# A decoder layer on one core: weight sums of column pair 1 moved behind a token split, down-projection sums moved two column pairs on, stores of f moved ahead

## What is computed

```python
h = rms_norm(x, pre_ffn_w[l]) * (1.0 + scale2) + shift2
u = causal_dwconv(h @ w_up[l], ffn_conv_w[l], ffn_conv_b[l])      # 1024 -> 2 * 2816, 3 taps
u_gate, u_val = jnp.split(u, 2, axis=-1)
f = (jax.nn.gelu(u_gate, approximate=True) * u_val) @ w_down[l]   # 2816 -> 1024
x = x + gate2 * rms_norm(f, post_ffn_w[l])
```

## Time and profile before

| | |
|---|---|
| median of 3 runs | 1133.82 us (1129.49 to 1134.27) |
| the profiled execution | 1129.23 us, of which 1127.2 us are its span |
| PE busy | 1075.1 us, 95% of the span |
| DVE busy | 871.6 us, 77% |
| ACT busy | 560.5 us, 50% |
| POOL busy | 253.3 us, 22% |
| mean granted TensorE clock | 0.983 |

### The profile page before, as it was taken

One profiled execution on the slowest core, in us unless ns is written; L12 is line 12 of the kernel. 1 busy time (PEld: TensorE's weight loads), 2 busy tenths in 40 slices (PEclk: granted clock), 3 DMA queues, 4 the chain that ended last, 5 costly groups with the idle time before them and its releaser, 6 DMA issues.

```text
span 1127.2 us, 14880 instructions
## 1 busy us (share of the span) xinstructions
PE 1075.1 (95%) x5096; PEld 865.0 (77%) x5096; DVE 871.6 (77%) x1121; ACT 560.5 (50%) x1012; POOL 253.3 (22%) x237
## 2 busy tenths in 40 slices
PE   4699999999998999889999999999999999999997
PEld 3578766666686888767888888888888888888885
DVE  5869677767559687799888888888888877776687
ACT  4821254545554556565554445445444545544453
POOL 2000011121125443133333333333333100000012
PEclk7799999999999999999999999999999999999999
DMA  9979411001134222235353535343433595623324
GB/s 345 321 245 318 139 38 38 20 20 38 57 114 133 92 94 75 76 93 165 115 167 112 167 112 167 109 164 118 153 107 123 206 391 196 213 94 96 100 85 168
DMA packets 117503, 157.40 MB, mean 140 GB/s; under 512 B 15308, under 2 KB 76237, under 8 KB 117453
## 3 DMA queue, kind: packets, MB, share of 16 engines
q1 hardware_dynamic: 117133, 155.69, 41.3%
q0 software_dynamic: 320, 1.06, 0.3%
HBM read 125.75 MB, written 30.98 MB: 139 GB/s over the span
## 4 chain that ended last, share of the span: by engine, by line
PE 77%; DVE 11%; ACT 4%; DMA 2%; issue 2%; POOL 1%; SPq 1%; DVEq 0%; POOLq 0%; ACTq 0%
PE ps L2451 33%; PE ps L2518 18%; PE ps L2121 18%; DVE big L1409 3%; DMA raw<-in_w_in_dram 2%; PE ps L2160 2%; PE ps L2186 1%; PE ps L2174 1%; DMA scratch<-in_rel_bias_dram 1%; PE ps L2291 1%; DVE w_lo L1450 1%; PE ps L2077 1%; PE ps L2219 1%; POOL st L766 1%; DVE a_lo L1743 0%
## 5 line engine op out<-in xcount | busy, mean ns | idle before, releaser
L2121 PE MATMUL ps<-a_hi,w_hi 128*128 128x512 f32 x416 | 141.9, 419 | 7.5 <-DVE a_lo L1469 3.8
L2121 PE MATMUL ps<-a_lo,w_hi 128*128 128x512 f32 x416 | 131.6, 395 | 0.0
L2121 PE MATMUL ps<-a_hi,w_lo 128*128 128x512 f32 x416 | 131.0, 393 | 0.0
L2518 PE MATMUL ps<-w_hi,a_hi 128*128 128x512 f32 x308 | 119.9, 389 | 0.2 <-DVE a_lo L1953 0.2
L2518 PE MATMUL ps<-w_lo,a_hi 128*128 128x512 f32 x308 | 119.8, 389 | 0.0
L2518 PE MATMUL ps<-w_hi,a_lo 128*128 128x512 f32 x308 | 119.8, 389 | 0.0
L1321 ACT ACTIVATE w_hi<-raw 128x512 fp32r<-128x512 f32 x77 | 48.7, 632 | 98.4 <-PE ps L2518 88.8
L2121 PEld LDWEIGHTS ps<-a_hi,w_hi 128*128 128x128 f32 x416 | 72.7, 191 | 29.4 <-issue 16.3
L2121 PEld LDWEIGHTS ps<-a_lo,w_hi 128*128 128x128 f32 x416 | 78.9, 190 | 17.7
L2121 PEld LDWEIGHTS ps<-a_hi,w_lo 128*128 128x128 f32 x416 | 78.7, 189 | 17.9
L1238 ACT ACTIVATE scratch<-ps 128x512 f32<-128x512 f32 x88 | 52.0, 593 | 80.6 <-PE ps L2451 80.5
(11 more groups left out here) (270 smaller groups left out, 2398.5 us busy)
## 6 DMA issues: line engine op xcount, KB each, us to landing
big<-in_w_ada_dram SPq DMA_DIRECT2D x20, 1024.0 KB, 8.8
raw<-in_w_up_dram SPq DMA_DIRECT2D x23, 512.0 KB, 5.0
big<-in_w_down_dram SPq DMA_DIRECT2D x22, 512.0 KB, 6.2
down_weight_sums<-big SPq DMA_DIRECT2D x22, 512.0 KB, 3.4
raw<-down_weight_sums SPq DMA_DIRECT2D x44, 256.0 KB, 2.8
ffn_hidden<-big SPq DMA_DIRECT2D x21, 512.0 KB, 2.6
big<-ffn_hidden SPq DMA_DIRECT2D x21, 512.0 KB, 7.5
big<-in_w_up_dram SPq DMA_DIRECT2D x20, 512.0 KB, 4.9
```

Of the source, the lines that this page charges most:

```text
L2121: mm = pe.matmul(out, lhs_of[a], rhs_of(b, j), start=first and p == 0, stop=last and p == 2)
L2518: mm = pe.matmul(bk, a[:, ts], rhs_op(s)[w], start=fresh and m == 0, stop=last and m == 2, skip_group_check=s // KH in (J6, J3, J7))
```

## The change

Three edits. POOL waits, before the weight sums of pair 1, until the low part of b22 REST is made. DVE makes the sums of w_down number 0 in pair 2 instead of pair 1; number 1 stays in pair 3. SP stores f of the pair before ahead of the stores and loads for the sums, in all pairs.

```diff
--- before.py
+++ after.py
@@ -658,12 +658,12 @@
                     sp.wait_ge(s_ul, weights_to(p, "a22"))
                     sp.wait_ge(s_us, 4 if first else p * 2 + 2)
                     load_pair(p + 2, par)
+                if not first:
+                    store_f(p - 1)
                 if par == 0 and not first:
                     store_sums(i - 1)
                 if par == 1 and not last:
                     load_sums(i)
-                if not first:
-                    store_f(p - 1)
@@ -858,6 +858,7 @@
+            pool.wait_ge(s_bl, splits_to("b22", REST))
             weight_sums(1, 1)
             with pool.Fori(1, FT // 2) as i:
                 for par in range(2):
@@ -1969,8 +1970,10 @@
             next_weights(1, 1)
             assemble(0, 0, 1)
 
-            up_pair(1, 1, sums=0)
-            with dve.Fori(1, FT // 2 - 1) as i:
+            up_pair(1, 1)
+            up_pair(2, 0, sums=0)
+            up_pair(3, 1, sums=1)
+            with dve.Fori(2, FT // 2 - 1) as i:
                 for par in range(2):
                     up_pair(i * 2 + par, par, sums=i if par else None)
             up_pair(FT - 2, 0, sums=KH - 1)
```

## The result

The changed kernel took 1134.27 us (median of 20 runs, 1131.97 to 1138.84), the kernel before beside it 1132.07 us (20 runs). The ratio estimated from all runs is 1.0025 with a 95% interval of 1.0015 to 1.0035: 2.8 us slower (1.7 to 4.0), within 0.5%. The two medians are 2.2 us apart; the interval holds both.

A forecast was written before the change was run, and what follows sets the result against it. PE, busy 95% of the span, bounds the kernel, so only its waits and low clock can be won. Terms -1.1 + 0.3 + 2.7 = +1.9 us, 1135.7 us with 4.6 us added for the median; range 1129.5 to 1141.0 us.

The forecast's parts named there:

- (a): Start of pair 0: POOL's sums leave 487 to 494 us; PE 2.5 us ahead, 1.8 more if clock stays up.
- (d): t2 of pair 2: without w_down sums in pair 1 its 2.27 us wait goes; start at 535.2 instead of 536.29.
- (g): Pair 20: load of last rows waits for the sums' landing; PE waits 2.7 us before pair 21's t2, bounds 0.5 to 5.
- (e): w_down sums in pair 2: 0.2 us cover the copy for t2 of pair 3; price 0, up to 1 us.
- (f): Odd pairs from 3: rows of w_down load only when f is ready; price 0 to 1.5 us, 0.3 taken.
- (b): t3 of pair 0: POOL's sums behind b22 REST stretch DVE; PE waits 3.6 us, 0.4 of the 4.3 us lead left.
- (c): b11 of pair 2: weights come late, start at 527.0 instead of 525.57, a loss of 1.4 us.
- the alternation does not bite: Rival, 6%: POOL's sums behind b22 REST mostly don't block DVE, no gap at t3; -2.8 us, 1131.0 us.
- The list of signs: Waits expected in the changed profile, including 3 to 4 us before pair 0's t3 and 2 to 4 before pair 21's t2.
- The end is covered: Rival, 12%: pair 20's two transfers take 2.7 us less than thought; change worth -0.8 us, 1133.0 us.
- slow landings: Rival, 15%: at the end stores of sums take 7 us instead of 3.5; +6.1 us, 1139.9 us, over 0.5% slower.

The follow-up runs named there:

- e2: Kernel before with only POOL's new wait (b22 REST) ahead of pair 1's weight sums; 1133.2 us, ratio 1.0022.
- e5: Changed kernel with POOL's four weight sums of pair 1 replaced by constant writes to the same places, leaving out part of the computation; executed once, 1129.28 us.
- e4: Kernel before with sums number 0 moved to pair 2 and POOL's wait, without the stores of f ahead; 1131.6 us, ratio 1.0011.
- e6: Changed kernel with SP's last entry (pair 20) in its old order, f behind the stores of sums; 1130.84 against 1131.24 us for the kernel before.
- e7: Changed kernel with the rows of w_down loaded ahead of the store of f again in odd pairs; 1131.8 us, ratio 1.0006.
- e10: e8 with the change's own POOL wait (b22 REST) for all four sums of pair 1; 1130.44 us, ratio 0.9993.
- e8: Kernel before with sums number 0 moved to pair 2 and f stored ahead in pair 2's SP entry alone, no POOL wait; 1129.68 against 1131.24 us.
- e1: Kernel before with only the w_down sums number 0 moved from pair 1 to pair 2; 1129.17 against 1130.34 us.
- e9: e8 with POOL's sums of pair 1 parted, two waiting for t1 MIDDLE and two for t2 LATE; 1126.19 us against 1130.83 for the kernel before.
- e11: The changed kernel itself executed once more, unchanged; 1134.03 us, the kernel before beside it 1130.86.
- e3: Kernel before with only the stores of f moved ahead in SP's list; 1136.83 us, ratio 1.0065.

## Why the prediction was right, and where it was off

The forecast was 1.9 us more than before, the measurement 2.8 (1.7 to 4.0), the first profile 2.65 in the stage. As a time it was 1135.7 us, and 1134.27 came: the 4.6 us that I had added for the median rested on three runs, and over 20 runs the median of the kernel before is 1132.07, 2.8 us above its profiled execution. I go through the terms with the first profile. The mechanisms of (a) to (d) and of (g) held; that the sum came within 1 us is partly luck, because the error of +0.94 us in (e) and (f) and that of -0.72 in (g) nearly cancel, and the clock behind two of the waits could have gone either way.

**(a) held.** Wait for t1: 1.57 us for 1.6 predicted, the 1.02 us gone. t1 starts at +13.83 for +16.43 before, 2.6 us sooner (2.5 predicted), and the 24 matmuls of t1 and t2 take 5.7 us at the full clock instead of 7.20.

**(b) held.** DVE's four instructions took 7.9 us for 8.0 predicted, the wait before t3 was 3.21 us for 3.6, and t3 starts at +28.73 for +29.07, 0.34 us sooner (0.4 predicted). e2 has the gap with this edit alone, and e5 shows its cause. The rival "the alternation does not bite" is ruled out.

**(c) held, with one sentence too sure.** b11 of pair 2 came 1.17 us later than before for 1.4 predicted. I wrote that a fall of the clock in the new gap only fills this wait. That is so in the change's second profile, in e2 and in e4 (b11 at +46.95). In these the clock was low for some 3 us. In e6, e7 and e10 it was low for more than 5 us, and b11 starts at +47.9 to +48.0: the fall then costs 1.0 us more than its cover.

**(d) held.** PE reached t2 of pair 4 at 579.53 - 1.24 - 484.67 = +93.62; before it was there at 56.48 + 2 x 19.05 = +94.58. So (a) to (d) gave 0.96 us for 1.1 predicted.

**(e) and (f) were mis-sized: 1.24 us for 0 + 0.3.** The place was right (pair 3, the rows of w_down), and the value lay inside the stated bounds of 0 to 1.5, though beyond the 1.0 that its own numbers give at most (2.9 us late less 1.9 covered). The list of signs names no wait there. DVE's sums of pair 3 start at 572.39 - 484.67 = +87.72 for +84.63 before, 3.1 us later, for some 2.2 predicted. The cover was not the 1.9 us that I had worked out either: PE came 0.96 us sooner than before, which leaves 0.9. But the four sums took 2.79 us instead of 3.76, because this time none of POOL's instructions fell beside them. 3.1 - 1.0 - 0.9 = 1.2. The part missed is in (e): I priced the sums in pair 2 at nothing because PE does not wait for them, and in (f) left the store of f at 560.04, where it was before, while by (d) PE is 1.1 us ahead. The chain above runs through DVE, and f of pair 2 is ready 0.96 us later (store at +81.19 for +80.23) with PE 0.96 ahead. The other runs show which edit does it: with the wait alone (e2) f of pair 2 is 1.2 us late and so is PE; with the sums moved and no wait (e8) PE is 2.2 us ahead at t2 of pair 4 and f only 0.4. e7 takes the load out from behind f, and the wait of PE is gone. The later odd pairs cost nothing at PE, as predicted.

**(g) was the largest term, as predicted: 1.98 us for 2.7, or more with the clock.** DVE's sums of pair 20 start at +413.84 for +409.64 before, 4.2 us later (4.5 predicted), and PE itself comes 0.5 us later than before, so 2.3 us were covered for 1.8. The second store of sums landed in 4.37 us (I had 3.5 and "somewhat more") and the load in 4.47 (5.4 taken): two errors that nearly cancel. What I left out is the clock behind this wait: in the second profile it fell and cost 1.6 us. e6 shows that the end carries the loss. "The end is covered" falls with the 1.98 us, and "slow landings" with the 4.37, where 6.6 were needed.

**The rest**, 0.4 us, is in no term: a product behind a wait runs its first matmuls slower. t2 of pair 4 and t2 of pair 21 take 2.89 and 2.90 us to the start of the next product, where 2.72 is the rule, with the granted clock at 1.00. -0.96 + 1.24 + 1.98 + 0.4 = 2.7.

By the Trainium skill, DMA: Bandwidth & Descriptors, section Anatomy of one DMA, both loads of rows together would take an estimated 4.4 us, from a fit for another queue. In pair 20 they took 4.85 us (893.63 to 898.48), with four loads of 256 KB issued behind them, in pair 3 5.86 (566.51 to 572.37), with f ahead of them and two loads of 512 KB behind: too low in both places, by 0.5 and 1.5 us, so the bounds from rows were needed.

What the prediction did not look for is what each edit is worth without the others. The stores ahead were priced by their two costs alone; e1 and e4 show what they prevent, a block of 0.9 us once the sums are moved, and e8 shows that one entry of the queue is enough for it.

## What to carry to other kernels

Moving a stall on a shared port to a later place won here where that place had some idle time (e9) and lost where it had none (e2, e10): count how many instructions with two SBUF inputs stand there in a row on the other engine before naming it. On a queue that keeps its order, put the transfer that somebody waits for ahead of one that waits itself, but entry by entry: the same swap that freed pair 2 put two landings in a row at the end. And price not only whether PE waits for a late engine, but what that engine's lateness hands to the next transfer.

## What the runs showed of the hardware

- The clock behind a wait is not fixed by the wait. Behind 3.21 to 3.23 us before t3 it fell to 0.50 in six of seven profiles (e2, e4, e6, e7, e10, e11) and not in one (the change's first); behind 1.98 us before t2 of pair 21 it stayed, behind 2.08 (e3) and 2.14 (e11) it fell. The two profiles of the change are of one kernel. Behind the same 3.14 us before t1 that the kernel before has the earlier trace rows, e1 kept 1.00 where the profiles of before, e3 and e8 fell to 0.50. And behind 2.27 us before t2 of pair 2 the kernel before kept 1.00, as e2 did behind 2.25, so the longer wait is not always the one that falls. A window of the kernel before, behind those 2.27 us:

```profile
536.30:538.30 2.00, 2.00 (x9) 1.65 (x10) 1.47 (x2) 2.00 (x3) 1.23 (x1) 1.00 0.00 0
```

- A fall also has two sizes. In e2, e4 and e11 the clock was low for some 3 us behind the wait before t3, in e6, e7 and e10 for 5 to 6, and behind the 3.73 us of e3 for 6. What decides whether it falls and for how long stays open. Waits of 2 to 3.2 us are priced best with both outcomes, here nothing, or 1.6 us behind 2.1 us of wait; e3's 3.73 us cost 3.0.
- GpSimd's writes of a constant (0.53 us for 128x512) did not stretch VectorE's instructions beside them, while each sum of the same size added 1.1 us to the one beside it (2.32 us for 1.22).
- One 512 KB transfer of SyncE's queue landed in 4.37 (a store), 4.47 and 5.32 us (loads) on the chains shown. That the difference comes from what else was in flight fits these places but was not tested.
